# Two loads of projection weights moved from SyncE's DMA queue to ScalarE's, and one expert slot released earlier

## The reference

```
x = first_block(x, ...)                      # two layers: token mixer and convolutional FFN
x = second_block(x, ...)                     # one layer:
  hl = rms_norm(xl) * (1 + sc) + sh          # also for 256 context tokens
  pl = hl @ w_in
  a = hgrn2_mixer(...)                       # gated linear recurrence
  b = rwkv7_mixer(...)                       # delta rule: s = s*w - (s@kk) ak + v k, both directions
  c = neighbourhood_attention(...)
  xl = xl + g1 * (concat([a, b, c]) @ w_out)     # the output projection
  h2 = rms_norm(xl) * (1 + sc2) + sh2
  xl = xl + g2 * hierarchical_moe(h2)        # router, then 32 experts, each gate, up and down
```

## Time and profile before

| | |
|---|---|
| time, median of 3 | 1808.15 us (1805.14 to 1809.33) |
| the profiled execution | 1807.72 us, of it the span 1805.9 us |
| PE busy | 1581.8 us, 88% |
| DVE, ACT, POOL busy | 852.1, 644.9 and 135.6 us |
| mean granted PE clock | 0.95 |
| read from HBM | 414.45 MB |

### The profile page before, as it was taken

How to read it: one execution, slowest core, us unless ns; L and a number is a source line. 1 busy time by engine, 2 the same in 40 slices (tenths; PEclk the granted TensorE clock), 3 DMA queues, 4 the chain that set the end, 5 groups by cost and what they waited for, 6 DMA issues and landing times.

```text
span 1805.9 us, 33575 instructions
## 1 busy us (share of the span) xinstructions
PE 1581.8 (88%) x14933; PEld 1273.8 (71%) x14933; DVE 852.1 (47%) x1147; ACT 644.9 (36%) x834; POOL 135.6 (8%) x105
## 2 busy tenths in 40 slices
PE   8999999999999999899998999978898666565566
PEld 6999998998799999899987887667654222212221
DVE  4445565665534456566656785885533011101111
ACT  4344444544344453454536223545512000000100
POOL 0600000000051000000002461000000000000000
PEclk9999999999999999999999999999999888887788
DMA  8553456755666525678542341100299999999998
GB/s 297 202 187 117 140 205 237 293 187 183 220 236 240 183 70 201 232 275 278 188 149 82 94 113 35 25 4 4 80 373 389 424 425 428 425 426 424 427 425 343
DMA packets 130265, 418.36 MB, mean 232 GB/s; under 512 B 14171, under 2 KB 35486, under 8 KB 111187
## 3 DMA queue, kind: packets, MB, share of 16 engines
q1 hardware_dynamic: 129698, 416.14, 60.8%
q10 hardware_dynamic: 432, 0.22, 0.0%
HBM read 414.45 MB, written 1.89 MB: 231 GB/s over the span
## 4 chain that ended last, share of the span: by engine, by line
PE 61%; DMA 16%; DVE 11%; ACT 5%; SPq 4%; issue 3%; DVEq 0%; ACTq 0%
PE ps_q L1374 18%; PE ps_p L1374 16%; DMA R<-w_exp_gate 12%; SPq L1267 4%; PE ps_q L1992 3%; PE ps_s L1489 3%; PE ps_t L1489 3%; DMA R<-w_exp_down 2%; ACT w_high L2057 2%; PE ps_p L1543 2%; PE ps_t L1543 2%; PE ps_s L1543 2%; DVE w_low L2539 1%; PE ps_q L1543 1%; DMA wring<-w_up 1%
## 5 line engine op out<-in xcount | busy, mean ns | idle before, releaser
L2539 DVE TENSOR_TENSOR w_low<-wring,w_high 128x2048 fp32r<-128x2048 f32 (+1 forms) x127 | 288.0, 2268 | 302.4 <-ACT w_high L2057 302.0
L2057 ACT ACTIVATE w_high<-wring 128x2048 fp32r<-128x2048 f32 (+1 forms) x127 | 236.2, 1860 | 331.8 <-PE ps_q L1374 151.5
L1992 PE MATMUL ps_q<-R 128*32 128x512 f32 x640 | 143.8, 721 | 113.3 <-DMA wring<-w_exp_up 69.9
L1992 PEld LDWEIGHTS ps_q<-R 128*32 128x32 f32 x640 | 35.7, 129 | 208.6 <-issue 132.4
L1374 PE MATMUL ps_q<-x_high,w_high 128*128 128x256 f32 x864 | 174.1, 283 | 3.6 <-DVEq L2590 3.6
L1374 PE MATMUL ps_q<-x_low,w_high 128*128 128x256 f32 x864 | 172.8, 282 | 0.0
L1374 PE MATMUL ps_q<-x_high,w_low 128*128 128x256 f32 x864 | 172.0, 280 | 0.0
L1374 PE MATMUL ps_p<-x_high,w_high 128*128 128x256 f32 x736 | 148.3, 283 | 4.2 <-DVEq L2590 4.2
L1374 PE MATMUL ps_p<-x_low,w_high 128*128 128x256 f32 x736 | 147.4, 282 | 0.0
L1374 PE MATMUL ps_p<-x_high,w_low 128*128 128x256 f32 x736 | 146.3, 280 | 0.0
L1992 PE MATMUL ps_q<-wring,R 128*32 128x512 f32 x384 | 143.5, 716 | 0.0
(11 more groups left out here) (789 smaller groups left out, 3062.1 us busy)
## 6 DMA issues: line engine op xcount, KB each, us to landing
wring<-w_in SPq DMA_DIRECT2D x29, 2048.0 KB, 7.9
R<-w_exp_up SPq DMA_DIRECT2D x24, 2048.0 KB, 37.3
R<-w_exp_down SPq DMA_DIRECT2D x24, 2048.0 KB, 44.0
wring<-w_up SPq DMA_DIRECT2D x22, 2048.0 KB, 8.0
R<-w_exp_gate SPq DMA_DIRECT2D x16, 2048.0 KB, 34.9
wring<-w_exp_gate SPq DMA_DIRECT2D x16, 2048.0 KB, 33.7
wring<-w_ada SPq DMA_DIRECT2D x12, 2048.0 KB, 11.1
wring<-w_down SPq DMA_DIRECT2D x10, 2048.0 KB, 7.8
```

The source lines that it names most:

```text
L1992: mm = pe.matmul(banks8[2 + which][q, :], xg[:, k, q], ww[u][:, k, :], start=k == 0, stop=k == KT - 1)
L2057: a.activation(high_of(l, job), half_block(l, job, wring), ACT.Copy).then_inc(w_high_ready, 1)
L2539: v.tensor_tensor(half_block(l, job, w_low), half_block(l, job, wring), high_of(l, job).bitcast(F32), ALU.subtract).then_inc(w_low_ready, 1)
```

## The change

Three edits. SP no longer waits for ("GT", 3) and no longer issues w_out; behind the two small loads it goes straight to the expert blocks. ACT issues w_out on its own queue, behind the steps of the mixer, of which the last is the taking out of ("GT", 3), and ahead of the taking out of ("mt", 0). DVE raises moe_used by 1 already behind the taking out of ("NN", 3), in the "products" of the last group, and by 2 in place of 3 behind ("GT", 3).

```diff
@@ SP
-            wait_full2(sp, ("GT", 3))
-            for half in range(2):
-                name, c, width = BLOCKS2[half]
-                sp.dma_start(w2(half), d[name][0].rearrange("(k p) n -> p k n", p=P)[:, :, c:c + width]).then_inc(loaded[half], 16)
@@ ACT
+            wait_emptied2(a, ("PH", 3))
+            for half in range(2):
+                name, c, width = BLOCKS2[half]
+                a.dma_start(w2(half), d[name][0].rearrange("(k p) n -> p k n", p=P)[:, :, c:c + width]).then_inc(loaded[half], 16)
             take(("mt", 0), mixT[:, 0:2, :], split=2)
@@ DVE
                     v.tensor_tensor(NN[:, g, :, :, :].rearrange("p a c t -> p (a c) t"), b3(("NN", g)), mask(1, dr), ALU.mult)\
                         .then_inc(dve_emptied2, 1)
+                    if g == 3:
+                        v.memset(st[:, 61:62], 0.0).then_inc(moe_used, 1)
@@ DVE
             wait_emptied2(v, ("GT", 3))
-            v.memset(st[:, 61:62], 0.0).then_inc(moe_used, 3)
+            v.memset(st[:, 61:62], 0.0).then_inc(moe_used, 2)
```

## The result

The changed kernel takes 1814.81 us in the median of 9 runs (1810.69 to 1818.13), against 1805.30 for the kernel before in 9 runs next to it. The ratio is 1.0038 with a 95% interval of 1.0028 to 1.0049, so the change costs 5 to 9 us, 6.9 by the ratio. The two medians lie further apart, 9.5 us, because the median of before lies 1.6 us under the mean of its nine runs; the mean times differ by 7.5. The forecast was 1815.2 and slower, 7.0 us over a median of 1808.15 in three runs.

What follows compares the result with a forecast made beforehand. PE's progress to block 12's release bounds the kernel, with a constant stream behind it. The terms 0.1 + 0 + 5.2 + 1.7 = 7.0 us later gave 1815.2 us; own range 1812 to 1818, 8 in 10 range 1806.5 to 1818.5.

Steps and rivals of the forecast that it cites:

- What bounds the kernel: Expert stream at the end: PE's release of block 12 sets the end; loading a first block earlier gains 0.
- The w_out issues on ACT: Ahead of ACT's taking out of ("mt", 0): both issues fit the 1.17 us gap, cost 0, else up to 1.0 us.
- Turns by packet: Where w_out on ACT's queue meets blocks 1 and 2 on SP's: queues alternate by packet, not by byte.
- some 540: w_out's half 0 at 1303.3: packets out of 1024 when blocks 1 and 2 start, leaving 30 on each engine.
- The clock: PE at mix_out(0): a low-clock spell of 3.4 us behind the stall loses half of it, 1.7 us; bounds 0 and 2.6.
- The stall of 5.2 us: PE ahead of mix_out(0): w_out's half 0 lands at 1317.2, wanted at 1311.93; bounds 0 and 6.6 us.
- the one from issue to first packet: Blocks 1 and 2 on SP's queue: first packets move 1.3 us after the issue, by 1303.3.
- the simple sum: Half 0's landing: 1300.1 plus 5.4, plus two blocks of 4.93, plus 1.8 to landing, gives 1317.2.
- Block 0 "meets no other load": Early block 0 in the mixer, issued near 1246: it has the engines to itself at 4 GB/s; gain 0.
- The 0.1 us of the sum: DVE behind NN of group 3: the extra memset that releases block 0 early costs 0.1 us, at most 0.69.
- a rival of 0.08: More than the stall: two low-clock spells, or queued PE instruction loads and ACT held; 10.2 us, about 1818.4 and over, chance 0.08.

Runs made afterwards that it cites:

- e4: Kernel before with block 0 issued early by SP in four paced pieces, each issued after the previous one landed; ratio 0.9996.
- e9: Kernel before with e4's paced early block 0, and SP waiting for w_out's half 0 to land before issuing half 1; ratio 0.9998.
- e10: Changed kernel with block 0 in four paced pieces and SP waiting for w_out's half 0 before issuing block 1; ratio 0.9990.
- e12: The same kernel as e10, measured once more; ratio 1.0000.
- e6: Changed kernel with ACT issuing half 1 of w_out ahead of half 0; ratio 1.0098, median 1824.38 us.
- e5: The changed kernel measured once more without any edit; ratio 1.0049.
- e1: Changed kernel with block 0's release put back behind GT 3, so only w_out's move to ACT's queue remains; ratio 1.0009.
- e2: Kernel before with only block 0 released and issued early by SP, ahead of its wait for GT 3; ratio 1.0017.
- e11: e2's kernel with block 0 loaded twice, the second load behind the landing of the first; ratio 1.0026.
- e3: Changed kernel with SP waiting for w_out's half 0 to land before it issues block 1; ratio 1.0016.
- e7: e2's kernel with block 0 in four loads of 4 KB rows, one behind the other without gaps; ratio 1.0021.

## Why the prediction was right, and where it was not

**What bounds the kernel: right.** Block 12's issue moved by 5.21 us and the span by 5.4. e4 and e9 show the other side: block 0 earlier, at no cost, gains nothing.

**The w_out issues on ACT: right.** No delay of the next taking out, in the profile and by e10 and e12.

**Turns by packet: right.** 93 packets of 16 KB went against 94 of 2 KB in 4 us of the changed kernel, and e6's half 0 landed after 23.9 us. (The prediction's "some 540" packets out by 1303.3 is 562 by its own figures, 312 and 1.3 us at 192 a us, so 29 and not 30 an engine; nothing hangs on it.)

**The clock: right in size, 1.7 us, but not as a fixed price.** In the changed kernel it came as forecast: behind the stall the clock was at 0.50 from 1316.4 to 1319.8, 3.4 us, all on mix_out(0). In e5 it was no second spell but one long one that had begun ahead of y_out. In e1 and e2 mix_out(0) ran partly at low clock with no stall ahead of it, for 6.23 and 6.41 us in place of 5.42, because the spell that began ahead of it lasted 6.8 us and not 3.4.

**The stall of 5.2 us: right in mechanism, wrong in size.** It measured 1.97 and 0.66 us. The term that was mis-sized is the one from issue to first packet. The prediction took 1.3 us, as for w_out on free engines (by the packets it was 1.1); block 1, issued while w_out kept all engines busy, needed 3.6. Of half 0's 1024 packets 764 were out by 1306 and 873 by 1307, so about 11 an engine were left when block 1 began, fewer than the 16 of blocks 1 and 2, so the simple sum, in which both blocks are served before half 0 is complete, did not hold. The margin is sharp: each packet that an engine still holds costs 0.7 us (its own 0.083 and the 0.616 of the large one that takes its turn). With 11 left half 0 landed after 15.2 us (changed), with 9 after 14.5 (e5), with 6 after 11.9 (e1), and a shift of 0.31 us between the two issues is what parts the first from the last. The trace of before had the hint: the small ACT load issued at 1344.13 sent its first packet at 1347.74, also 3.6 us later, and I read in it only the turns.

**Block 0 "meets no other load": wrong, and this is the step that failed.** The 0.1 us of the sum is for the memset; the load itself stood at nothing, and cost 3.62 us in the profile, 3.0 in time (e2). Of the 3.62, 2.50 is the tear, and the rest goes with the 3.4 us of low clock behind it; in e2 and e5, without that spell, the distance grew by 2.6 and 2.7. The load that it meets is the one that a list of transfers does not make one think of: instructions. The packets of 1250:1252 in the kernel before are a single line:

```profile
q8 instruction: 1, 0.02, 4.1%
```

One such packet of 16 KB comes about every 4 us in the mixer. That is 4 GB/s: the 4 GB/s of the earlier trace rows, in which the prediction read that block 0 meets no load, are this load. The Trainium skill ("Runtime: NRT & Kernel Launch", section "Instruction fetch mechanics") says that each engine's instructions are refilled in blocks of 16 KiB, 256 instructions, through a DMA queue of its own. The size agrees with the row (0.02 MB), and from one packet to the next between 1220 and 1244 PE and PEld began 228 to 272 instructions, 252 in the mean, so I read q8 as PE's queue. The Trainium skill calls the cost mostly hidden; here it is not, as the tears show.

That it is PE's refill which is late can be read from the packets. In the changed kernel, for 1241.5:1248.6 and 1248.6:1248.7, q8 has no packet in the first window and one in the second (q14 is another queue of instructions, with packets of 8 KB):

```profile
q1 hardware_dynamic: 97, 1.59, 61.3%
q14 instruction: 1, 0.01, 0.3%
...
q8 instruction: 1, 0.02, 56.2%
```

The packet before it began at 1241.40, so 7.2 us lie between the two, and PE went on 2.29 us after the late one began. In all the kernels the packets from 1235 to 1251 are 3.4 to 4.7 us apart, but for the late one in each of those with the burst, which came 6.4 to 7.4 us behind the one before it; PE went on 2.3 to 2.4 us after it each time. The second tear of e11 is the same (7.15 us, then 2.26). The idles of over 1 us in the quiet part of the mixer that end with no releaser, and the idle inside y_out, end 2.2 to 2.8 us after such a packet too. The runs agree with this: the tear sits at the same matmul in the changed kernel, e2, e3, e5, e6 and e7, inside a job without waits, appears with the load (e2), stays with small rows (e7), doubles with two loads (e11) and goes with gaps (e4). The prediction had instruction loads that queue behind data only as a rival of 0.08, for the meeting of the two queues near 1303 and not for block 0.

So the forecast of 7.0 us met the 7.36 of the profile with wrong parts: 0.1 + 5.2 + 1.7 was forecast, and 3.6 + 2.0 + 1.7 was measured. That the total agreed is luck. So is part of the hit on 1815.2: it stood on a median of before of 1808.15, and that median in nine runs was 1805.30.

**What stays open.** Why the first packet of a second queue needs 3.6 us on busy engines. It was 3.6 with 2 KB packets ahead (block 1) and with 16 KB packets ahead (the small load), which looks like a fixed amount of bytes or time in line and not a number of packets; a slow making of descriptors for w_out is not excluded by a run that would separate them. PE's refill was late by some 3 us behind block 0, where a turn behind one 16 KB packet would be 0.6; whether that is the same delay no run tests. And the parts do not add: e1 and e2 give 1.0009 and 1.0017, the whole 1.0038 and 1.0049. The profiles point to the sharp margin, since the early block 0 also moves the issue of block 1 forward by 0.31 us against w_out; no run held that shift alone fixed. How long the clock stays low near mix_out(0) also differs from run to run, by up to 3 us of time.

## What to carry to other kernels

A load that has the engines to itself in the list of transfers still shares them with the instruction refills of a busy engine: look for the instruction packets in a "free" window before you put two megabytes in one burst there, and pace the load. Moving a load to a second queue gives up its place ahead of others: if it was first in line and its consumer has only a few us of slack, small rows against large ones lose their turn one for one. Ask of an early load first who waits for it: here nobody did, since the queue dries up and PE releases the next slot.

## What the runs showed of the hardware that I had not expected

- A transfer issued on an idle queue while another queue keeps the 16 engines busy sent its first packet 3.5 to 3.6 us after its issue began (changed kernel, e1, e5, e6, and the small ACT load of before), against 1.0 to 1.1 on free engines (block 0 and w_out).
- 2 MB in one burst beside a PE in a dense run of small matmuls held PE up for 1.7 to 2.8 us, in each of the six kernels that had it; in four pieces with gaps it did not. Row sizes of 16 and 4 KB made no clear difference (1.7 to 2.8 and 1.96 us).
- PE's instructions came in one 16 KB packet about every 4 us there. Beside the 2 MB the packet came 6.4 to 7.4 us behind the one before it, and PE went on 2.3 to 2.4 us after the packet had begun.
- Between 1220 and 1243 PE stands still for 1.1 to 1.7 us about every 4 us even with quiet DMA engines, inside or at the start of jobs that wait for nothing.
- The granted clock dropped to 0.50 behind some of these idles and not behind others of the same length (2.50 us in the changed kernel: yes; 2.51 in e2 and 2.78 in e5: no).
